# Hybrid decoder trunk: the last MLP's weight-block sums on GpSimd in place of VectorE, p7's ahead of p6's

## The reference

```python
def sq_relu_mlp(xn, w1, w2):
    return jnp.square(jax.nn.relu(xn @ w1)) @ w2

for layer in range(DEPTH):          # DEPTH = 2
    ...                             # mixer and cross attention
    ff = sq_relu_mlp(rmsnorm(h, norm_mlp[layer]), mlp_w1[layer], mlp_w2[layer])
    h = h + ff
return rmsnorm(h, norm_final)
```

## Time and profile before

| | |
|---|---|
| median of 3 runs | 2365.22 us (2364.89 to 2366.28) |
| profiled execution | 2366.67 us, of which the span of the instructions is 2364.8 us |
| TensorE busy | 2352.0 us, 99% of the span |
| VectorE busy | 1727.7 us, 73% |
| ScalarE busy | 1264.9 us, 53% |
| GpSimd busy | 362.1 us, 15% |
| mean granted clock of TensorE | 0.999 of full speed |

### The profile page before, as it was taken

One profiled execution on the slowest core, in us unless ns is written; L12 is line 12 of the kernel. 1 busy time (PEld: TensorE's weight loads), 2 busy tenths in 40 slices (PEclk: granted clock), 3 DMA queues, 4 the chain that ended last, 5 costly groups with the idle time before them and its releaser, 6 DMA issues.

```text
span 2364.8 us, 30981 instructions
## 1 busy us (share of the span) xinstructions
PE 2352.0 (99%) x12302; PEld 1989.0 (84%) x12302; DVE 1727.7 (73%) x2138; ACT 1264.9 (53%) x1661; POOL 362.1 (15%) x470
## 2 busy tenths in 40 slices
PE   9999999999999999999999999999999999999998
PEld 7888888889888888888888888889888888888887
DVE  5546554556688888788888647566688888888887
ACT  7544445546655555544445445556656555655554
POOL 0033120002781000145443100000000000000001
PEclk9999999999999999999999999999999999999999
DMA  9755565564756655587777968954656656656653
GB/s 355 266 176 183 176 210 173 169 186 154 232 179 203 212 180 185 195 241 244 255 248 226 279 232 243 291 196 146 212 178 218 203 175 221 199 177 197 213 160 142
DMA packets 342240, 492.63 MB, mean 208 GB/s; under 512 B 19512, under 2 KB 185248, under 8 KB 341968
## 3 DMA queue, kind: packets, MB, share of 16 engines
q1 hardware_dynamic: 316800, 464.04, 61.1%
q0 software_dynamic: 4032, 14.02, 1.9%
q10 hardware_dynamic: 21264, 12.59, 1.7%
HBM read 475.72 MB, written 19.08 MB: 209 GB/s over the span
## 4 chain that ended last, share of the span: by engine, by line
PE 94%; DVE 3%; ACT 1%; issue 1%; DMA 0%; ACTq 0%; SPq 0%; DVEq 0%
PE acc L1239 14%; PE acc L726 13%; PE acc L728 13%; PE acc L727 13%; PE acc L1248 7%; PE acc L1164 4%; PE acc L1278 3%; PE acc L1279 3%; PE acc L1277 3%; PE acc L1172 2%; PE at L1219 2%; PE at L1221 2%; PE at L1222 2%; PE at L813 2%; DVE wlo L2089 2%; PE tp L789 1%
## 5 line engine op out<-in xcount | busy, mean ns | idle before, releaser
L2089 DVE TENSOR_TENSOR wlo<-raw,whi 128x1024 fp32r<-128x1024 f32 x456 | 596.6, 1315 | 389.5 <-ACT whi L1447 386.6
L1447 ACT ACTIVATE whi<-raw 128x1024 fp32r<-128x1024 f32 x472 | 496.6, 1059 | 464.9 <-PE acc L728 301.5
L1836 ACT ACTIVATE whi<-raw 128x1024 fp32r<-128x1024 f32 x264 | 275.6, 1056 | 320.0 <-PE acc L1248 165.3
L2558 DVE TENSOR_TENSOR wlo<-raw,whi 128x1024 fp32r<-128x1024 f32 x280 | 339.4, 1222 | 104.7 <-ACT whi L1836 98.9
L1239 PE MATMUL acc<-x,whi 128*128 128x512 f32 x1408 | 334.6, 390 | 0.0
L1239 PEld LDWEIGHTS acc<-x,whi 128*128 128x128 f32 x1408 | 261.5, 188 | 52.5
L726 PE MATMUL acc<-whi,yt_hi 128*128 128x512 f32 x704 | 278.8, 396 | 0.7 <-DVE h L2137 0.5
L728 PE MATMUL acc<-whi,yt_lo 128*128 128x512 f32 x704 | 274.4, 390 | 0.0
L727 PE MATMUL acc<-wlo,yt_hi 128*128 128x512 f32 x704 | 274.1, 389 | 0.0
L2993 POOL TENSOR_TENSOR arena<-arena 128x32 f32<-128x32 f32 (+5 forms) x275 | 204.2, 743 | 414.6 <-DMA arena<-fp_d 280.3
L726 PE MATMUL acc<-whi,x 128*128 128x512 f32 x672 | 265.8, 396 | 0.0
(11 more groups left out here) (279 smaller groups left out, 3617.0 us busy)
## 6 DMA issues: line engine op xcount, KB each, us to landing
raw<-in_mlp_w SPq DMA_DIRECT2D x212, 1024.0 KB, 5.7
raw<-in_ab_w_in SPq DMA_DIRECT2D x56, 1024.0 KB, 5.0
arena<-in_mlp_w SPq DMA_DIRECT2D x72, 512.0 KB, 4.9
raw<-in_cd_w_in SPq DMA_DIRECT2D x32, 1024.0 KB, 6.2
raw<-in_ab_w_out SPq DMA_DIRECT2D x16, 1024.0 KB, 5.0
raw<-in_cd_w_out SPq DMA_DIRECT2D x16, 1024.0 KB, 6.9
raw<-in_xa_wkv SPq DMA_DIRECT2D x14, 1024.0 KB, 11.8
raw<-in_xa_wq SPq DMA_DIRECT2D x16, 512.0 KB, 4.9
```

Of the source, the lines that this page charges most:

```text
L1447: act.activation(split_weights(whi, kind, p.n["half"] + i), half_weights(raw, kind, i), ACT.Copy)\
L1836: act.activation(split_weights(whi, kind, p.n["half"]), half_weights(raw, kind, i), ACT.Copy)\
L2089: dve.tensor_tensor(split_weights(wlo, kind, n), half_weights(raw, kind, i), split_weights(whi, kind, n).bitcast(F32), ALU.subtract).then_ ...
L2558: dve.tensor_tensor(split_weights(wlo, kind, n), half_weights(raw, kind, i), split_weights(whi, kind, n).bitcast(F32), ALU.subtract).then_ ...
```

## The change

For layer 1 alone, the eight sums of a group leave VectorE's list. GpSimd gets a loop over the seven groups with the same sums, after its last work for the mixer and before its wait for the last split. The order in the loop is p5, p7, p6, p4, where VectorE had p5, p6, p7, p4; so the counts that ScalarE waits for are now looked up by layer. Each sum waits for its slot's landing, for the split that reads the slot before it is overwritten, and each waits for the one before it. Layer 0 keeps the sums on VectorE.

```diff
+T_COUNT = ({"p5": 1, "p6": 3, "p7": 5, "p4": 7}, {"p5": 1, "p7": 3, "p6": 5, "p4": 7})
...
-                    act.wait_ge(t_sum, p.at("s") * 8 + {"p5": 1, "p6": 3, "p7": 5, "p4": 7}[name] + j)
+                    act.wait_ge(t_sum, p.at("s") * 8 + T_COUNT[layer][name] + j)
...
-                t1(layer, 1)
+                if layer == 0:
+                    t1(layer, 1)
...
+            def weight_sum(g, nth, o, a, j, landed, read=None):
+
+                pool.wait_ge(s_in[landed[0]], 32 * landed[1])
+                if read is not None:
+                    pool.wait_ge(lo_ready, read)
+                o, a = (sraw[1][n][j] for n in (o, a))
+                pool.tensor_tensor(o, o, a, ALU.add).then_inc(t_sum, 1)
+                pool.wait_ge(t_sum, 8 * g + nth + j)
+
+            for c in range(GROUPS[1]):
+                g = GROUPS[0] + c
+                own = S_AT[1] + FIRST_HALVES + (c - 1) * CHUNK_HALVES
+                after = own + CHUNK_HALVES
+                for j in range(2):
+                    weight_sum(g, 1, 0, 1, j, (1, g + 1), own + PLACE_OF["p1", j] + 1)
+                for j in range(2):
+                    weight_sum(g, 3, 1, 2, j, (2, 2 * g + 1))
+                for j in range(2):
+                    weight_sum(g, 5, 0, 2, j, (2, 2 * g + 1), after + PLACE_OF["p5", j] + 1)
+                for j in range(2):
+                    weight_sum(g, 7, 0, 2, j, (2, 2 * g + 2), after + PLACE_OF["p6", j] + 1)
```

More of the change, by code:

```diff
@@ L2579, in up_first @@
                 s_lo(layer, "p5", 1)
-                t2(layer, 0)
+                if layer == 0:
+                    t2(layer, 0)
                 plain_lo(0, 6)
                 plain_lo(0, 7)
-                t2(layer, 1)
+                if layer == 0:
+                    t2(layer, 1)
                 s_lo(layer, "p3", 0)
@@ L2586, in up_first @@
                 evict(layer, 1, "p5", at[:, 1, :], ((1, 3),))
-                t3(layer, 0)
+                if layer == 0:
+                    t3(layer, 0)
                 p.bump("unit")
@@ L2600, in up_second @@
                 s_lo(layer, "p6", 1)
-                t3(layer, 1)
+                if layer == 0:
+                    t3(layer, 1)
                 evict(layer, 2, "p3", at[:, 1, :], ((0, 3),))
@@ L2611, in up_second @@
                 head_lo(1, 1)
-                t4(layer, 0)
+                if layer == 0:
+                    t4(layer, 0)
                 s_lo(layer, "p2", 0)
@@ L2616, in up_second @@
                 plain_lo(1, 7)
-                t4(layer, 1)
+                if layer == 0:
+                    t4(layer, 1)
                 evict(layer, 4, "p7", at[:, 0, :], ((1, 2), (1, 3)))
@@ L2643, in down @@
                     s_lo(layer, "p1", 1)
-                    t1(layer, 0)
+                    if layer == 0:
+                        t1(layer, 0)
                 plain_lo(2, 6)
```

## The result

The changed kernel takes 2414.12 us (median of four runs, 2412.51 to 2415.48) against 2365.75 for the kernel before on the same chip: a ratio of 1.0204 (95% interval 1.0192 to 1.0216), 48 us slower. I had forecast 2401 and a range up to 2412. Direction, mechanism and the three places were right; the loss is a third larger than worked out.

A forecast was written before the change was run, and what follows sets the result against it. TensorE was taken to bound the kernel, busy 2352.0 of 2364.8 us. Losses of 3.2 + 0.5 + 1.4 = 5.1 us a group, times 7 = 36, on 2366.7 gave 2402.7, less 1.4: 2401 us, range 2382 to 2412.

The forecast's parts named there:

- mechanism: VectorE two-input and GpSimd instructions on SBUF never run together; each sum returns as about 2.3 us of VectorE standstill.
- Place C: p4's sums, behind slot 2's reload: they delay p7's first split, so TensorE waits 1.4 us a group.
- the granted clock: TensorE's clock over the last MLP stage: forecast to stay at 1.00, adding nothing to the sum.
- No gain from unloading VectorE: Last MLP stage: TensorE never waits there, so taking 68 us of sums off VectorE gives nothing.
- place A: End of the down unit: p5's second and p7's sums delay split (2,7) and the accumulator; 3.2 us a group.
- Rival 1: Last MLP stage: sums and splits run side by side, so not slower, time stays at 2365; chance 0.05.
- rival 2: p7's pair does not chain at the down unit's end: smaller loss, 20 us, 2385; chance 0.17.
- Place B: Behind p5's splits: p6's sums hold up the split of (0,6), making TensorE 0.5 us late a group.
- Rival 3: Clock falls after standstills, five microseconds a group costing 2.3 us each: 16 more, 2417; chance 0.13 with other additions.
- bound for the length of a hold: How long a sum keeps VectorE out: 2.28 us taken; shortest about 1.8 (2380), longest 2.43 (2408).
- The new order of p7 and p6: At the down unit's end: p7's two sums follow p5's at once, chaining holds that delay split (2,7).

The follow-up runs named there:

- spread version: Kernel before, with all 56 sums on GpSimd, each let go where VectorE's next splits have time to spare: 2367.43 us, ratio 1.0003.
- C alone: The spread version, but with p4's sums let go as in the changed kernel: 2380.12 us, ratio 1.0059.

## Why the prediction was right, and where it was not

**The steps that failed are two terms of the sum.** Place C was put at 1.4 us a group and measured 2.1 to 2.3, because the reloaded slot's landing was taken at 4.8 us and took 6.4 to 7.1. And the fall of the granted clock, put at nothing in the sum, cost some 5 us in all. The rest of the walk held.

**No gain from unloading VectorE: right.** The spread version shows it in a run, at 1.0003.

**The mechanism: right, and shown rather than argued.** An addition on GpSimd costs as much with VectorE's work unchanged, a fill holds nothing up, and a copy holds for its own, shorter length. The held-up split took 3.45 us where I had 3.42, L2657 and L2659 took 2.89 and 2.77, and the walk through place A at 2.28 us a hold gave the lateness of the split of (2,7) to 0.1 us. Rival 1, with the time unchanged, and rival 2, with p7's pair not chained at A, are both refuted by the rows of place A. GpSimd's sums came out inside the 2.4 to 3.4 us that I had named, and TensorE's idle time lies where I had put it and nowhere else.

**Place A: 3.2 forecast, 2.35 + 1.12 = 3.5 of waits measured. Place B: 0.5 forecast, 0.6 measured** (4 us over seven groups when alone). Told by the distance from group to group, the two together cost 89.15 - 85.33 = 3.8 us where I had 3.7. With both left and p4's sums late, the kernel took 2394; by my terms that is 7 x 3.7 = 26 on 2366, 2392, and two falls of the clock come on top.

**Place C: 1.4 forecast, 2.1 to 2.3 measured.** This term was mis-sized. I took 4.8 us to landing, the median of the earlier trace rows, for the reload of slot 2, though my own sentence had it go out right behind a slab load. In the kernel before, the pair went out 4.6 us behind the slab load and landed after 3.9 to 4.8 us; in the changed kernel it went out 0.5 us behind it and took 6.4 to 7.1:

```profile
DMA to landing us min/median/max: 3.9/4.3/4.8
```

This row is the kernel before's, for the pair at 2028.43. That the 1 MB ahead of the pair makes the difference is read from these rows; no run issued the pair at the same moment without it. The maximum of 8.0 in the earlier trace rows was the warning: it belongs to the last of four such loads in a row. So p4's first sum came behind the split of (1,3) and not behind that of (1,2), one VectorE instruction nearer to p7's split, and the second sum met that split itself. C alone cost 14 us, and issuing the load six us earlier removed it.

**The granted clock: put at 1.00, and wrong.** The walk left it out, with the reason that the gaps are shorter than the idle stretch ahead of the fall in the tail. The clock fell all the same, 0.2 us after the end of a wait of 2.35 us (1922.95 behind 1922.77). Rival 3 had this, with too large a price: five microseconds at the lower level a group, 2.3 us net. Measured were 3.4 us, of which 0.6 is left at A, since the slower matmuls use up the wait for the accumulator that follows. At C, where nothing follows to absorb it, 1.6 is left: that group took 93.7 us where a fall at A alone makes 92.1 and none 91.5. Six falls at A and one at C make some 5 us.

**The sum.** 3.8 for A and B, 2.3 for C and 0.7 for the clock make 6.8 a group where the prediction had 5.1; times seven 48 for 36, and the medians differ by 48. (The two profiled spans differ by 46.7, since the changed kernel's was 1.6 us ahead when the first standstill came.) Of the twelve missing microseconds some 6 are C's, 5 the clock's and 1 is A's and B's. The range failed for the same reason: it had a bound for the length of a hold, which was the one number that was known, and none for the landing time, though its own row went from 3.8 to 8.0.

**The new order of p7 and p6: neither harm nor help.** I had blamed it for the chain at A. With p6 first on GpSimd the chain forms at another place, at the same 48 us.

**Still open:** what makes the clock fall. After A it fell in two groups of seven when C was absent (two kernels), in six with C present as well, and never with C or B alone. With the old order on GpSimd, which has no standstill at A, it fell eight times, at B and at C. Which part of the pattern decides was not told apart.

## What to carry to other kernels

Work moved from VectorE to GpSimd isn't off VectorE: an addition of two blocks in SBUF keeps VectorE's two-input instructions out for about twice the time that VectorE itself would need, so place each one where the next VectorE results have 2.3 us to spare, and never two in a row. Where TensorE is busy without a gap, such a move can gain nothing and can lose. And a load's landing time is read for the place in the queue that it will have after the change, with what is issued just ahead of it, not as the median of the line.

## What was not expected of the hardware

The clock fell for 3.4 us behind standstills as short as 2.3 us in a TensorE that was otherwise busy, and not behind all of them: there are 21 standstills in the changed kernel, seven at each place, and seven falls, none of them at B. GpSimd's fills of 1024 elements (954 ns) left every split at 1214 to 1227 ns, while its copy, with one input, kept splits out for its whole length like an addition: they ended 1.07 to 1.08 us after it. Of VectorE's own work only instructions with two inputs in SBUF were held: the eviction from an accumulator at 1968.05 took its usual 0.74 us while p4's second sum was running.
